# A fused attention and recurrence layer on one Trainium2 core: accumulator passes, first sums and early tiles rearranged

## What is computed

```python
mod = silu(c) @ w_ada + b_ada                  # (4096) x (4096, 12288): shift, scale, gate_res
h = rms(x) * norm_w * (1 + scale) + shift      # (256, 4096)
q, k, v, z_a, f_logit, x_r, z_r = split(h @ w_in)      # six groups of 2048 columns, one of 16
att = forgetting_attention(rms(q), rms(k), v, log_sigmoid(f_logit + b_f))   # 16 heads of 128
y_a = (att * silu(z_a)) @ w_br_attn
y_r = (rg_lru(conv(x_r)) * silu(z_r)) @ w_br_rnn       # 16 recurrent blocks of 128
g_a, g_r = split(sigmoid(h @ w_gate + b_gate))
y = x + gate_res * ((g_a * y_a + g_r * y_r) @ w_out)
```

## Time and profile before

| | |
|---|---|
| median of 3 runs | 2589.74 us (2588.42 to 2589.97) |
| the profiled execution | 2589.3 us, of it the span 2587.5 us |
| PE, PEld busy | 2547.5 us (98%), 2106.7 us (81%) |
| DVE, ACT, POOL busy | 1942.9 us (75%), 1358.2 us (52%), 39.9 us (2%) |
| DMA | 700.85 MB, mean 271 GB/s |
| chain that ended last | PE 92%, DVE 3%, issue 2% |

### The profile page before, as it was taken

One profiled execution on the slowest core, in us unless ns is written; L12 is line 12 of the kernel. 1 busy time (PEld: TensorE's weight loads), 2 busy tenths in 40 slices (PEclk: granted clock), 3 DMA queues, 4 the chain that ended last, 5 costly groups with the idle time before them and its releaser, 6 DMA issues.

```text
span 2587.5 us, 31118 instructions
## 1 busy us (share of the span) xinstructions
PE 2547.5 (98%) x11469; PEld 2106.7 (81%) x11469; DVE 1942.9 (75%) x2019; ACT 1358.2 (52%) x1598; POOL 39.9 (2%) x58
## 2 busy tenths in 40 slices
PE   5999999999999999999999999999999999999999
PEld 4777888888888888888888888888888888888887
DVE  6999999999989576675666666668787878754544
ACT  6676557555444456654666666544444344433333
POOL 0000000000000000220000000000000000000000
PEclk9999999999999999999999999999999999999999
DMA  9999999999999576556666666689898989667675
GB/s 333 349 319 335 341 362 345 369 361 350 369 329 343 165 205 193 152 159 188 195 196 194 199 194 198 196 307 353 314 350 312 349 313 349 207 206 228 208 228 171
DMA packets 379452, 700.85 MB, mean 271 GB/s; under 512 B 28082, under 2 KB 83620, under 8 KB 379044
## 3 DMA queue, kind: packets, MB, share of 16 engines
q1 hardware_dynamic: 378784, 698.72, 81.4%
q10 hardware_dynamic: 516, 0.13, 0.0%
HBM read 694.55 MB, written 4.21 MB: 270 GB/s over the span
## 4 chain that ended last, share of the span: by engine, by line
PE 92%; DVE 3%; issue 2%; ACT 1%; DMA 1%; SPq 0%; ACTq 0%; DVEq 0%
PE ps_acc L1331 27%; PE ps_acc L1333 27%; PE ps_acc L1342 27%; PE ps_t L1331 3%; PE ps_t L1333 3%; PE ps_t L1342 3%; DVE store L1062 1%; DVE acc L893 1%; DVE acc_first L893 1%; DVE w_lo L884 1%; PE ps_t L1452 1%; PE ps_t L1406 0%; DMA ada_ring<-in_w_ada 0%; ACT w_hi L671 0%; DMA land<-in_w_in 0%
## 5 line engine op out<-in xcount | busy, mean ns | idle before, releaser
L671 ACT ACTIVATE w_hi<-land 128x1024 fp32r<-128x1024 f32 x896 | 949.1, 1061 | 1102.2 <-PE ps_acc L1333 792.0
L884 DVE TENSOR_TENSOR w_lo<-land,w_hi 128x1024 fp32r<-128x1024 f32 x896 | 1094.4, 1222 | 537.7 <-ACT w_hi L671 534.1
L1331 PE MATMUL ps_acc<-w_hi,h_hi 128*128 128x512 f32 x2684 | 1049.6, 391 | 3.9 <-ACT w_hi L671 2.3
L1333 PE MATMUL ps_acc<-w_hi,h_lo 128*128 128x512 f32 x2684 | 1044.7, 389 | 0.0
L1342 PE MATMUL ps_acc<-w_lo,h_hi 128*128 128x512 f32 x2684 | 718.4, 389 | 0.9 <-DVE w_lo L884 0.9
L1331 PEld LDWEIGHTS ps_acc<-w_hi,h_hi 128*128 128x128 f32 x2684 | 503.9, 188 | 112.9 <-ACT ps_acc L802 4.3
L1342 PEld LDWEIGHTS ps_acc<-w_lo,h_hi 128*128 128x128 f32 x2684 | 503.1, 188 | 107.7 <-DVE w_lo L884 3.0
L1333 PEld LDWEIGHTS ps_acc<-w_hi,h_lo 128*128 128x128 f32 x2684 | 503.9, 188 | 103.2
L893 DVE SCALAR_TENSOR_TENSOR acc<-ada_ring,cvec,acc 128x1024 f32<-128x1024 f32 (+1 forms) x303 | 309.2, 1020 | 8.5 <-DMA ada_ring<-in_w_ada 5.2
L1209 DVE SCALAR_TENSOR_TENSOR racc<-res_land,cvec,racc 128x1024 f32<-128x1024 f32 x124 | 158.6, 1279 | 0.5 <-DMA res_land<-in_w_ada 0.3
L1331 PE MATMUL ps_t<-w_hi,h_hi 128*128 128x512 f32 x380 | 148.6, 391 | 1.7 <-ACT ps_t L802 1.6
(11 more groups left out here) (228 smaller groups left out, 1492.2 us busy)
## 6 DMA issues: line engine op xcount, KB each, us to landing
land<-in_w_in SPq DMA_DIRECT2D x384, 512.0 KB, 5.3
land<-in_w_gate SPq DMA_DIRECT2D x256, 512.0 KB, 4.6
ada_ring<-in_w_ada SPq DMA_DIRECT2D x160, 512.0 KB, 6.0
res_land<-in_w_ada SPq DMA_DIRECT2D x128, 512.0 KB, 7.7
land<-in_w_out SPq DMA_DIRECT2D x128, 512.0 KB, 4.4
ada_ring<-in_w_ada SPq DMA_DIRECT2D x152, 256.0 KB, 4.9
land<-in_w_br_attn SPq DMA_DIRECT2D x64, 512.0 KB, 4.2
land<-in_w_br_rnn SPq DMA_DIRECT2D x64, 512.0 KB, 5.4
```

The lines of the kernel that those rows point to most:

```text
L671: act.activation(w_hi[:, n % PARTS], land[:, n % LAND], ACT.Copy).then_inc(hi_rdy, 1)
L884: dve.tensor_tensor(w_lo[:, n % PARTS], land[:, n % LAND], w_hi[:, n % PARTS].bitcast(F32), ALU.subtract).then_inc(split_done, 1)
L1331: pe.matmul(sums[:, t], l_hi(kk, t), w_hi[:, n % PARTS, kk], start=first and kk == 0 and not added, stop=False, skip_group_check=added)
L1333: ins = pe.matmul(sums[:, t], l_lo(kk, t), w_hi[:, n % PARTS, kk], start=False, stop=False, skip_group_check=added)
```

## The change

Six edits. (1) Which jobs are seeded is now a fixed rule: in the middle passes up to `THIRD_END`, ScalarE has every job of accumulators 0 and 1, VectorE every job of accumulator 2; 86 jobs are seeded. (2) Group 0 is summed in two sums, even and odd rows apart, added before the last tile. (3) Ten tiles instead of four go into `ada_first` slots, and SP sends every tile at `ada_pace`; tiles 1 to 6 are used up to one unit earlier. (4) Doubles come 10 tiles in 11 units, not 7 in 8; so the last tile is used in unit 277, not 284, and `wave_plan` gives 178 jobs. (5) On VectorE a singles tile's first row now stands right behind `lo(n)`, its second behind the empties and the groups' work. (6) `N_HEAD` is bounded below by `N_A - 39` and is now 345; `RG_START[0]` by `N_A + 11` and is now 395.

```diff
-FIRST_ACC = 6
+FIRST_ACC = 6, 7
...
-EARLY = 4
+EARLY_SLOT = 0, 1, 2, 3, 8, 9, 10, 11, 12, 13
+EARLY = len(EARLY_SLOT)
...
-ADA_PACE = (4, 5), (7, 8)
+ADA_PACE = (4, 5), (10, 11)
...
-def ada_slot(i):
-
-    return min(i, 3) if i < EARLY + RING - 1 else ada_pace(i)
...
-    return max(min(i + 1, 8), ada_pace(i) - 1)
+    return max((i + 3) // 2 if i < 7 else 0, ada_pace(i) - 1)
...
+def seeded(j):
+
+
+    kind, index, u0, units, _ = JOBS[j]
+    if kind != "w" or index[1] or index[2] or u0 + units > THIRD_END:
+        return False
+    return ACC_OF[j] < ACCS
+
+
+SEEDED = [j for j in range(len(JOBS)) if seeded(j)]
...
-N_HEAD = max(N_RQK + 4, last_unit(FINAL["v", 3]) + 3)
+N_HEAD = max(N_RQK + 4, last_unit(FINAL["v", 3]) + 3, N_A - 39)
...
-RG_START = [N_HEADS_END + 3 + RG_EVERY * n for n in range(BLOCKS)]
+RG_START = [max(N_HEADS_END + 3, N_A + 11) + RG_EVERY * n for n in range(BLOCKS)]
...
                 if i < EARLY:
-                    sp_.wait_ge(ada_used, 2 * i + 2)
-                    dst, landed_sem = ada_first[:, i].rearrange("p t s n -> p (t s n)"), ada_first_in[i]
+                    slot = EARLY_SLOT[i]
+                    sp_.wait_ge(ada_used, 2 * slot + 2)
+                    dst, landed_sem = ada_first[:, slot].rearrange("p t s n -> p (t s n)"), ada_first_in[slot]
...
+                if a == FIRST_TILES - 1:
+                    dve.wait_ge(ada_used, ADA_T - 2)
+                    st.did(dve.tensor_tensor(flat[0], flat[0], flat[1], ALU.add))
+                    st.sync()
                 for r in range(2):
                     t = 2 * a + r
                     if t < ADA_T - 1:
-                        ada_row(acc_first[:].rearrange("p s n -> p (s n)"),
-                                ada_first[:, a, r].rearrange("p s n -> p (s n)"), t, t)
+                        ada_row(flat[r], ada_first[:, a, r].rearrange("p s n -> p (s n)"), t, t - 1, first=a == 0)
...
                 if n >= PARTS:
                     lo(n)
+
+                for i in ada_at.get(n, []):
+                    if SIZES[tile_group(i)] == 1:
+                        ada(i, 0)
+                        if len(ada_at[n]) > 1:
+                            ada(i, 1)
                 for j in EMPTY_AT.get(n, []):
...
                 for i in ada_at.get(n, []):
-                    ada(i)
+                    if SIZES[tile_group(i)] == 1 and len(ada_at[n]) == 1:
+                        ada(i, 1)
+                    elif SIZES[tile_group(i)] == 2:
+                        ada(i, 0)
```

More of the change, by code:

```diff
@@ L195 @@
 LAST_THIRD = max(j for j in range(len(JOBS)) if ACC_OF[j] == ACCS)
-def share_passes():
-    per_unit = 2.27
-    vector, scalar = [0.96] * N_A, [0.89] * N_A
-    for i in range(TILES):
-        vector[ada_use(i)] += 1.04
-    for g in range(1, GROUPS):
-        u, size = group_last(g), SIZES[g]
-        for at, vec, sca in ((u + 1, 0.5, 0.45), (group_at(g, TURN_AT), 1.1, 0), (group_at(g, SCALE_AT), 0, 1.5),
-                             (group_at(g, LOW_AT), 0.5, 0)):
-            vector[at] += vec * size
-            scalar[at] += sca * size
-    v = s = 0.0
-    seeded = []
-    ends = {last_unit(j): j for j in range(N_W_JOBS)}
-    for u in range(N_A):
-        v, s = max(v + vector[u] - per_unit, 0), max(s + scalar[u] - per_unit, 0)
-        j = ends.get(u - 2)
-        if j is None:
-            continue
-        if JOBS[j][1][1]:
-            s += 0.87
-        elif (JOBS[j][1][2] or JOBS[j][2] + JOBS[j][3] > THIRD_END or v + 1 <= max(VECTOR_MOST, s + 1.74)):
-            v += 1
-        else:
-            s += 1.74
-            seeded.append(j)
-    return seeded
-SEEDED = share_passes()
+def seeded(j):
[4 more added lines that the diff above has]
+SEEDED = [j for j in range(len(JOBS)) if seeded(j)]
 FREED = []
@@ L358, in build @@
         wide = lambda g: [P, 2, SIZES[g] * CHANNELS]
-        acc_first = at("acc_first", wide(0), F32, sums_at(FIRST_ACC))
+        acc_first = [at(f"acc_first{r}", wide(0), F32, r_hi + u * 2 * K) for r, u in enumerate(FIRST_ACC)]
         acc = [None] + [at(f"acc{g}", wide(g), F32, sums_at(g)) for g in range(1, GROUPS)]
@@ L590, in _ @@
             for i in range(TILES):
-                ada_at.setdefault(ada_slot(i), []).append(i)
+                ada_at.setdefault(ada_pace(i), []).append(i)
             b_gate_v = b_gate.rearrange("(a n) -> a n", a=1)
@@ L885, in lo, with ada_row @@
                                   ALU.subtract).then_inc(split_done, 1)
-            def ada_row(sums, src, t, done):
-                if t == 0:
-                    ins = dve.tensor_scalar(sums, src, cvec[:, 0:1], None, ALU.mult)
+            def ada_row(sums, src, t, done, first=False):
+                if t == 0 or first:
+                    ins = dve.tensor_scalar(sums, src, cvec[:, t:t + 1], None, ALU.mult)
                 else:
@@ L897, in ada_first_tile @@
                 dve.wait_ge(ada_first_in[a], 32 if a < FIRST_TILES - 1 else 16)
+                flat = [sums[:].rearrange("p s n -> p (s n)") for sums in acc_first]
+                if a == FIRST_TILES - 1:
+                    dve.wait_ge(ada_used, ADA_T - 2)
+                    st.did(dve.tensor_tensor(flat[0], flat[0], flat[1], ALU.add))
+                    st.sync()
                 for r in range(2):
@@ L905, in ada_first_tile, with ada @@
                     for part in (slice(0, P), slice(P, 2 * P)):
-                        ada_row(acc_first[:, :, part], ada_first[:, a, r, :, part], t, t)
-            def ada(i):
+                        ada_row(acc_first[0][:, :, part], ada_first[:, a, r, :, part], t, t)
+            def ada(i, row):
                 g = tile_group(i)
@@ L911, in ada @@
                 if i < EARLY:
-                    dve.wait_ge(ada_first_in[i], 64)
-                    src = ada_first[:, i].rearrange("p t s n -> p (t s n)")
+                    dve.wait_ge(ada_first_in[EARLY_SLOT[i]], 64)
+                    src = ada_first[:, EARLY_SLOT[i]].rearrange("p t s n -> p (t s n)")
                 else:
@@ L917, in ada @@
                     src = ada_ring[:, b % RING].rearrange("p s n -> p (s n)")
-                src = src.rearrange("p (t n) -> p t n", t=rows)
-                for r in range(rows):
-                    ada_row(acc[g][:].rearrange("p s n -> p (s n)"), src[:, r], (i - TILE_AT[g]) * rows + r,
-                            ADA_DONE[i] - rows + r)
+                if row < rows:
+                    ada_row(acc[g][:].rearrange("p s n -> p (s n)"), src.rearrange("p (t n) -> p t n", t=rows)[:, row],
+                            (i - TILE_AT[g]) * rows + row, ADA_DONE[i] - rows + row)
             def mod_columns(g, k0, k1, sums, *signal):
@@ L1359, in first_sums @@
                 for s in range(2):
-                    ins = pe.matmul(first_columns(s, kk), acc_first[:, s, kk * P:(kk + 1) * P], ones_r[:].bitcast(F32),
+                    ins = pe.matmul(first_columns(s, kk), acc_first[0][:, s, kk * P:(kk + 1) * P], ones_r[:].bitcast(F32),
                                     start=True, stop=True)
```

1 line of the change is left out of this document (removed).

## The result

The changed kernel takes 2574.73 us (median of 4 runs, 2574.59 to 2574.96), the kernel before beside it 2589.56 (2588.42 to 2589.97): ratio 0.9944, 95% interval 0.9932 to 0.9956. That is 14.8 us less; 12.4 were forecast. The profiled execution took 2574.6 us, its span 2572.8.

The account below looks back on a forecast made before the run. TensorE is busy nearly throughout, so only its gaps can be won; VectorE was taken as the bound in units 24 to 97. Terms 1.3 + 10.5 - 1.5 + 2.0 = 12.3 us gave about 2577.3 us, range 2572.5 to 2584.5.

Parts of the forecast that it names:

- First sums: Start of the kernel: two sums shorten VectorE's rows, so the first column sums start earlier; 1.3 us won, bounds 0 and 2.0.
- Early tiles and passes together: Units 1 to 102: earlier weights and fewer VectorE passes win back 10.5 us lost, less 1.5 us of stalls left.
- the 2.5 us of cover: One-unit jobs: VectorE's `empty` on accumulator 2 is done about 2.5 us before TensorE needs it.
- Split rows: Units 24 to 97: an empty between two rows of a tile saves VectorE 14 x 0.115 = 1.6 us.
- Doubles: Units 98 to 283: 10 tiles in 11 units need 368 GB/s; nothing won, as no gap is there now.
- a sign of being wrong: In the doubles: `w_hi` late for weights would show the prediction wrong.
- The rival of the DMAs: Doubles, units 98 to 277: DMAs fall short of 368 GB/s, so slower, 2602 us at 350 GB/s; chance 0.06.
- Heads: Among the heads: the gap from a sigmoid's table load between head steps goes; 2.0 us won, from 0 to 2.4.
- Blocks: Blocks' ends meet the gate jobs in another phase; taken as 0, one meeting bounded by 2 us.
- Half only: Strips: empties on accumulator 2 and groups' work coincide, stalls move and 5 us stay; 2581 to 2584 us, chance 0.20.
- No change that can be told: ScalarE late at groups' passes, or new head collisions, give 5 to 8 us back; 2584.5 to 2590 us, chance 0.09.

Follow-up runs that it names:

- x3: Changed kernel with doubles back at 7 tiles in 8 units, heads from unit 350 and blocks from 400 as before: 2581.32 us.
- x4: Changed kernel with heads from unit 350 and blocks from unit 400 as before, doubles left at the new pace: 2575.69 us.
- x5: Changed kernel with four early tiles, the old slots and tiles used as late as before: 2577.62 us.
- x6: Changed kernel with both rows of a singles tile together behind the empties and the groups' work: 2576.67 us.
- x11: Changed kernel without VectorE's addition of the two first sums, which TensorE adds with more small matmuls: 2575.81 us.
- x2: Changed kernel with the old planner of middle passes, which leaves VectorE more of them: 2582.65 us.
- x8: Changed kernel with doubles at one tile in every unit, asking the DMAs for 386 GB/s: 2577.63 us.
- x9: Changed kernel with VectorE's turning of a singles group's sums right behind `lo(n)`, ahead of the row and the empty: 2574.06 us.
- x10: Changed kernel with heads from unit 347 and blocks from 405, so a sigmoid falls between two full head steps: 2577.61 us.
- x7: Kernel before with only the new rule for the middle passes: 2583.27 us, beside 2588.98 for the kernel before.
- x1: Changed kernel with all 32 rows of group 0 in one sum again: 2576.10 us.

## Why the prediction came out as it did

The sign, the mechanism of most terms and the range were right; the sum was 2.4 us short. The blocks' phase was put at nothing and brought 1.5, the first sums brought 0.7 more than their term, the heads 0.2 and the end of the span 0.4 more; the early tiles and passes together brought 0.5 less. Step by step, forecast then measured:

*First sums, 1.3: 2.04, mis-sized by a bound that was none.* VectorE's half was right: timeline of DVE in the changed kernel:

```profile
21.46 16.85 DVE L866 SCALAR_TENSOR_TENSOR acc_first<-ada_first,cvec,acc_first 128x512 f32<-128x512 f32 x24
38.41 0.69 DVE L874 TENSOR_TENSOR acc_first<-acc_first,acc_first 128x512 f32<-128x512 f32 x1
39.14 1.74 DVE L866 SCALAR_TENSOR_TENSOR acc_first<-ada_first,cvec,acc_first 128x512 f32<-128x512 f32 x3
```

24 rows in 16.85 us, 0.702 each instead of 0.794; 2.2 us saved. What failed is "it can't start before about 41.35", from the transposes' end at 41.4. PE in the changed kernel, and one window of PE in before and in after:

```profile
36.78 3.22 PE L1469 MATMUL ps_t<-ident 128*128 128x128 f32 x28
40.63 0.68 PE L1345 MATMUL ps_c<-ones_r,acc_first 128*128 128x128 f32 x4 [0.63 <-DVE acc_first L866]
```

```profile
35.00:39.00 4.00, 4.00 (x24) 0.57 1.08 360
```

```profile
35.00:39.00 4.00, 4.00 (x37) 1.00 1.09 361
```

The profile of before had its clock at 0.57 in just these 4 us, and the transposes I read there were slow ones. Without it they end at 40.0 and VectorE is the limit again. I had not looked at the clock at that place. The runs show both cases: where a half-clock stretch begins at 35 to 36 us (x3, x4, x5, x6, x11) the first sums start at 41.2 to 41.4, my bound; without it (after, x2, x8, x9, x10) at 40.4 to 40.7. It is 0.7 us.

*Early tiles and passes together, 9.0: 8.5* (2.2 in units 1 to 24, 5.8 in 25 to 98, 0.5 up to 290). The size was right, and stalls of 2.0 instead of 1.5 us are left. x5 and x7 show the two causes apart: the early tiles give 2.0 in units 1 to 24, the rule alone 5.6 of the 5.8 behind them. VectorE's busy share of 96% came out as worked, but not its saving: 11.9 us less were forecast, and by the windows under x2 it needs 7.2 less (207.9 to 200.7). With its short waits counted it stands at 98% of the 204.5 us. That was enough to bring it under TensorE's 202.7, with 2.0 us to spare where 7.8 were forecast. The stall that replaced the old one is another than I named: not TensorE waiting for an `empty` on accumulator 2, but ScalarE waiting for `modc` behind an `empty`, and the seed behind that. That no wait for an `empty` shows fits the 2.5 us of cover, which no run tests.

*Split rows: 1.6 us less of VectorE's work was forecast, none came.* Fewer rows stand right behind the row they need, 43 instead of 61, but each such wait is about 0.10 us instead of 0.035, so VectorE's waits for its own rows rose from 2.1 to 4.3 us. The prediction took the cost of a dependence from the old kernel and didn't count what the new order would do to it. x6 shows what is left of the cover: 2.8 us more of VectorE's need, and TensorE pays 2.2 of it.

*Doubles, 0: 0.1* (of the 0.5 just counted up to unit 290, 0.4 lies at unit 102, in the wake of the strips). 367 GB/s, and waits for weights that end at ScalarE. These waits, 17.4 us of them, were named as a sign of being wrong; it was a bad sign, since none reached TensorE. The rival of the DMAs shows only where units ask for more than the 375 GB/s that x8 got.

*Heads, 2.0: 2.24,* by the mechanism named (x10). *Blocks, 0, bounded by 2: 1.53* (x4). The bound was good and the value at its wrong end. The profile of before has two gaps of 0.48 and 0.49 us there, so there was something to be won; I had read only the heads' gap. That the new phase would miss them was luck: nothing in the prediction says why it should.

"Half only" failed on the 2.0 us of stalls left. "No change that can be told" failed too: ScalarE was busy 157.8 of 206 us, and TensorE stood for it twice, 0.66 and 0.22 us. Single terms don't add up: undoing one each (x1, x2, x4, x5, x6) costs 1.4 + 7.9 + 1.0 + 2.9 + 1.9 = 15.1 us, more than the 14.8 that all bring, though the heads' 2.2 are not even among them; some is the clock (see the last section), some is counted in two, since VectorE's slack serves several. Still open are how the part of x2's 7.9 us beyond VectorE's load divides, what makes a pair of rows 0.07 us dearer in the new code, and why the new rule on the old plan stops TensorE at unit 140.

## What to carry to other kernels

Before a bound is read from where one engine's work ends, look at the granted clock of that very stretch, and of small stretches, not of the page's slices. Where two engines hand partial sums to each other, a split by accumulator that keeps each sum on one engine may win more than a split that balances their loads, since it takes away the waits between them. To see whether an engine has cover to give, take the same units before and after, not the same window, add its own short waits to its busy time, and compare the sum with what the bound engine needs for these units: a busy share of 96% stood here for an engine with 2 us to spare and for one 5 us over. And price an experiment's "as before" against the old code itself, since a helper that was rewritten can carry a cost of its own.
